# Spacing the fill matmuls anew at the head of each pair of heads, and staging the first later block through ScalarE

## What is computed

```python
hn = rms_norm(h, norm_mix_pre[l])
p = hn @ w_in[l]
p_rw, p_ret, g_rw, g_ret = _split(p, IN_SIZES)
y_rw = rwkv7_mixer(p_rw, ...)         # below
y_ret = retention_mixer(p_ret, positions)

# rwkv7_mixer, for each head, over the tokens:
kk = kk / jnp.maximum(jnp.sqrt(jnp.sum(kk * kk, axis=-1, keepdims=True)), 1e-12)
k = k * (1.0 + (a - 1.0) * k_a)
sa = jnp.einsum('bhvk,bhk->bhv', S, -kk_t)
S = S * w_t + sa[..., None] * (kk_t * a_t) + v_t[..., None] * k_t
y = jnp.einsum('bhvk,bhk->bhv', S, r_t)
bonus = jnp.sum(r * k * r_k, axis=-1, keepdims=True) * v
```

## Time and profile before

| | |
|---|---|
| median of three runs (range) | 2453.03 us (2448.63 to 2453.11) |
| the profiled execution | 2453.11 us, span 2451.3 us |
| busy: PE, DVE, POOL, ACT | 97%, 56%, 32%, 27% of the span |
| mean granted PE clock | 0.992 of full speed |
| fills (L608, L613, L615) | 1920 matmuls, 779 us busy |

### The profile page before, as it was taken

One profiled execution on the slowest core, in us unless ns is written; L12 is line 12 of the kernel. 1 busy time (PEld: TensorE's weight loads), 2 busy tenths in 40 slices (PEclk: granted clock), 3 DMA queues, 4 the chain that ended last, 5 costly groups with the idle time before them and its releaser, 6 DMA issues.

```text
span 2451.3 us, 33679 instructions
## 1 busy us (share of the span) xinstructions
PE 2377.4 (97%) x12944; PEld 1922.5 (78%) x12944; DVE 1370.6 (56%) x1562; ACT 660.1 (27%) x1064; POOL 790.9 (32%) x420
## 2 busy tenths in 40 slices
PE   7999999999999999899999999999999999999997
PEld 5788878887888788787787788888878787777775
DVE  7744374437444653676638654455451387657766
ACT  4311121112112111343224211111122445114541
POOL 2311221123123214212465433333334445422164
PEclk9999999999999999999999999999999999999998
DMA  3111211111112114654444211111124333221123
GB/s 140 58 61 44 70 52 61 52 61 53 51 52 70 61 46 149 197 175 156 158 151 134 81 43 47 47 47 47 43 60 145 120 120 100 70 63 35 35 78 112
DMA packets 61904, 205.22 MB, mean 84 GB/s; under 512 B 6240, under 2 KB 10464, under 8 KB 61152
## 3 DMA queue, kind: packets, MB, share of 16 engines
q1 hardware_dynamic: 40560, 138.76, 18.2%
q10 hardware_dynamic: 21232, 64.80, 7.2%
HBM read 167.36 MB, written 36.18 MB: 83 GB/s over the span
## 4 chain that ended last, share of the span: by engine, by line
PE 83%; DVE 10%; DVEq 2%; ACT 2%; issue 1%; POOLq 0%; DMA 0%; POOL 0%; ACTq 0%
PE psg L476 10%; PE psg L481 9%; PE psg L480 9%; PE psg L615 5%; PE psg L613 5%; PE psg L608 5%; PE psa L704 1%; PE psg L1186 1%; PE psg L1179 1%; PE psg L1184 1%; PE psb L693 1%; PE psg L1223 1%; PE psg L1229 1%; PE psg L1227 1%; PE psb L700 1%
## 5 line engine op out<-in xcount | busy, mean ns | idle before, releaser
L401 POOL CAST whi<-wraw 128x1024 fp32r<-128x1024 f32 (+1 forms) x176 | 195.2, 1109 | 1437.1 <-PE psg L608 551.1
L403 POOL TENSOR_TENSOR wlo<-wraw,whi 128x1024 fp32r<-128x1024 f32 (+1 forms) x176 | 457.2, 2598 | 25.4 <-issue 0.2
L476 PE MATMUL psg<-xhi,whi 128*128 128x512 f32 x1008 | 402.6, 399 | 3.5 <-issue 1.9
L481 PE MATMUL psg<-xhi,wlo 128*128 128x512 f32 x1008 | 397.5, 394 | 0.0
L480 PE MATMUL psg<-xlo,whi 128*128 128x512 f32 x1008 | 396.0, 393 | 0.0
L615 PE MATMUL psg<-xhi,wlo 128*128 128x512 f32 x640 | 261.2, 408 | 0.0
L608 PE MATMUL psg<-xhi,whi 128*128 128x512 f32 x640 | 259.3, 405 | 0.0
L613 PE MATMUL psg<-xlo,whi 128*128 128x512 f32 x640 | 258.5, 404 | 0.0
L476 PEld LDWEIGHTS psg<-xhi,whi 128*128 128x128 f32 x1008 | 189.2, 188 | 49.6 <-issue 5.0
L481 PEld LDWEIGHTS psg<-xhi,wlo 128*128 128x128 f32 x1008 | 189.2, 188 | 48.2
L480 PEld LDWEIGHTS psg<-xlo,whi 128*128 128x128 f32 x1008 | 189.2, 188 | 45.9 <-issue 0.7
(11 more groups left out here) (612 smaller groups left out, 4821.5 us busy)
## 6 DMA issues: line engine op xcount, KB each, us to landing
wraw<-w SPq DMA_DIRECT2D x224, 512.0 KB, 3.6
later_scratch<-stage ACTq DMA_DIRECT2D x40, 512.0 KB, 2.6
xres<-xt ACTq DMA_DIRECT2D x4, 1024.0 KB, 11.6
RV<-later_scratch SPq DMA_DIRECT2D x4, 1024.0 KB, 11.6
RG<-later_scratch SPq DMA_DIRECT2D x4, 1024.0 KB, 5.7
later_scratch<-rstage ACTq DMA_DIRECT2D x8, 512.0 KB, 2.7
mgr<-later_scratch ACTq DMA_DIRECT2D x8, 512.0 KB, 3.6
mgt<-later_scratch ACTq DMA_DIRECT2D x8, 512.0 KB, 4.5
```

The source lines that it names most:

```text
L401: pool.tensor_copy(whi[:, u, 0:width], wraw[:, u, 0:width])
L403: pool.tensor_tensor(wlo[:, u, 0:width], wraw[:, u, 0:width], whi[:, u, 0:width].bitcast(F32), ALU.subtract).then_inc(w_ready, 1)
L476: mm = pe.matmul(ps[:, cols], whi[:, slot, w_cols], rhs_hi(k, cols), start=(k == 0), stop=False)
L481: mm = pe.matmul(ps[:, cols], wlo[:, slot, w_cols], rhs_hi(k, cols), start=False, stop=(k == kts - 1))
```

## The change

PE's 83 fills at the head of a pair, 36 before the wait on `hd_exp`, 14 before that on `rk_prod` and 33 before that on `rw_prep`, become 10, 22 and 51.

Block 0 takes another way out of PSUM. ScalarE copies it raw from `psg[0]` to `stage` (`put_first`), behind its last exponential of the head. VectorE multiplies `stage` by `factor` in place (`staged_half`), in group 0 behind `XM` of levels 1 and 2, in place of `normed_half(0, ...)` at the head of the group. The store of block 0 is issued behind `M` of level 3. In group 0 the halves of block 1 move from levels 3 and 4 to levels 4 and 5, and its store behind the levels. ScalarE gets a wait on `pp_ready` at the start of a pair.

```diff
@@ PE
-                fill(36)
+                fill(10)
                 pe.wait_ge(sem("hd_exp"), 2 * i + 1)
                 spread(TM).then_inc(sem("hd_rep"), 1)
-                fill(14)
+                fill(22)
                 pe.wait_ge(sem("rk_prod"), i + 1)
                 sum_rows(psb, M_BLK, TM).then_inc(sem("bonus_sum"), 1)
-                fill(33)
+                fill(51)
                 pe.wait_ge(sem("rw_prep"), i + 1)
@@ VectorE
+                def staged_half(half):
+
+                    cols = slice(half * HALF, (half + 1) * HALF)
+                    if half == 0:
+                        v.wait_ge(g_free[0], 8 * i + 6)
+                    mm = tt(stage[:, cols], stage[:, cols], factor[:, cols], MUL)
+                    if half:
+                        mm.then_inc(sem("first_normed"), 1)
...
                 tt(BON[:, :], flat(psb), V[:, :], MUL).then_inc(sem("rw_prep"), 1)
-                for half in range(2):
-                    normed_half(0, half)
                 for g in range(GROUPS):
...
-                        if lv in (3, 4):
-                            normed_half(2 * g + 1, lv - 3)
+                        if g == 0 and lv in (1, 2):
+                            staged_half(lv - 1)
+                        if lv in ((3, 4) if g else (4, 5)):
+                            normed_half(2 * g + 1, lv - (3 if g else 4))
@@ ScalarE
+                def put_first():
+                    s.wait_ge(sem("stored1"), 80 * i + 16)
+                    s.wait_ge(g_full, T_RW + RW_T * i + 7)
+                    act(stage[:, :], psg[0][:, :], CP).then_inc(g_free[0], 1)
+
+                s.wait_ge(sem("pp_ready"), i + 2)
...
                 act(SG[:, :], SG[:, :], EXP, scale=-C0).then_inc(sem("exp_ready"), 1)
-                store_later(0)
+                put_first()
                 for g in range(GROUPS):
...
-                        if lv == 4:
+                        if g == 0 and lv == 3:
+                            s.wait_ge(sem("first_normed"), i + 1)
+                            store_later(0)
+                        if g and lv == 4:
                             store_later(2 * g + 1)
+                    if g == 0:
+                        store_later(1)
```

## The result

The changed kernel takes 2474.12 us (median of four runs, 2473.2 to 2476.04) against 2453.07 before: ratio 1.0091, interval 1.0074 to 1.0108, so 18 to 26 us slower. A second set beside other kernels, with the label `again`, gave 2472.37 us, ratio 1.0086 (1.0072 to 1.0100). The profiled execution took 2471.75 us, span 2470.0, mean granted clock 0.990.

The account below looks back on a forecast made before the run. PE, busy 97% of the span, was taken to bound the kernel. Shift 12.8 + clock 4.8 - drops 3.4 + 0 + collision 4.0 = +18.2 us on 2453.11 gave 2471 us, range 2462 to 2475.

Parts of the forecast that it names:

- the clock: Head of each pair: low clock on the fills behind PE's idle time, 1.2 us per pair, 4.8 in all.
- the collision: Level 1, group 0: staged half waits for GpSimd's subtraction, L693 starts 1.0 us late per pair, 4.0 in all.
- the shift: Head of each pair: PE waits 5.7 us for TM, group 0 starts 3.2 us later, 12.8 in all.
- the drops taken away: Group 0: three drops of the granted clock behind the BON wait, 1.13 us each, disappear; 3.4 us less.
- The halves at the head of group 0: Head of group 0: taking the two normed_half(0, ...) away is worth 0 to PE.
- a stretched product: Level 1 of group 0: the staged half takes 1.9 us under GpSimd's subtraction, making L693 0.15 us late.
- The stores: Stores of blocks 0 and 1 in group 0: their later issue costs 0, with 0.2 us of cover.
- (b): Rival, chance 0.06: no wait at hd_exp; the BON waits and three drops are pure gain, 2439 us.
- (c): Rival, chance 0.07: GpSimd's split misses the mixing of V, hd_exp comes 2.2 us earlier, about 2457 us.
- (a): Rival, chance 0.27: level-1 half only stretched or ahead of GpSimd, 0 to 0.6 us, about 2467 to 2468.

Follow-up runs that it names:

- warm: Changed kernel plus 24 extra matmuls, whose result nobody reads, after the tenth fill, so PE is busy while it waits for TM: 2464.80 us, ratio 1.0050.
- fills: Kernel before with only the fills moved to 10/22/51, block 0 leaving PSUM as before: 2466.44 us, ratio 1.0056.
- stage23: Changed kernel with fills back at 36/14/33 and staged halves at levels 2 and 3 in place of 1 and 2: 2452.47 us, ratio 0.9997.
- lv23: Changed kernel with its two staged halves behind XM of levels 2 and 3 in place of 1 and 2: 2467.56 us, ratio 1.0058.
- hold: Kernel before, but GpSimd waits for rw_prep of the pair before it splits the weights of block f=2: 2437.39 us, ratio 0.9933.

## Where the prediction was off, and what it had right

The direction and the mechanism were right at each step, but one term was too small, and the range ended too low for it. The medians, 2474.1 and 2472.4, are 1 to 3 us above the 2471 forecast, and the ratio of the first set, put on 2453, reads 2475.4: just past the upper end of 2475.

That the profiled execution, at 2471.75 us, came within 1 us of the forecast is luck. At the head and in group 0, where the whole sum plays, it lost 21.7 us against the 18.2 forecast; it was 3.1 us quicker elsewhere, for which the sum has no term. The 3.5 between 18.2 and 21.7 are 2.6 from the clock, 0.8 from the collision and 0.3 from the shift, less 0.2 from the drops taken away.

- *The shift.* Forecast +3.2 us per pair, measured 3.27 (warm). The signal for `TM` did not move, PE stood 5.6 us before it, and the wait for `BON` went.
- *The clock: the step that failed, by its size.* "Bounds 0 and 1.55, I take 1.2." It was 1.3, 2.2, 2.6 and 1.4 us in the four pairs, 7.4 in place of 4.8, and two of the four lie outside the bounds. The upper bound took for granted that a low stretch lasts 3.4 us, as those behind the short waits in group 0 did. Behind 5.6 us of idle time it lasted 6.8 us in pairs 1 and 2, and in pair 2 PE ran 5.4 us of work at 0.50, in one piece. With PE kept busy in the wait (`warm`) the 7.4 are gone and the shift stays. With the term at 7.4 the sum is 12.8 + 7.4 - 3.4 + 4.0 = +20.8, and the time 2474. Why the stretch is 3.4 us long behind one such wait and 6.8 behind the next stays open.
- *The drops taken away.* Forecast -3.4; `fills`, where nothing else touches group 0, gives -3.6.
- *The halves at the head of group 0.* Forecast 0; `stage23` gives 0.
- *The collision at level 1.* Forecast 1.0 per pair, measured 1.2, the upper bound. L693 lists 0.91 of wait, counted from the modelled end of the fill before it. By the starts it comes 1.31 us behind that fill, where it came 0.24 behind it before: 1.07 of the 1.2. The alternative, a stretched product, would have been 0.15. VectorE's half began 0.14 us behind GpSimd and lasted to 124.27, when GpSimd was done at 123.73 which leaves 0.54 of its own 0.68. The rule of the Trainium skill, "SBUF — State Buffer", section "Who interferes with whom", that the later of the two is blocked until the earlier is done, agrees with this trace to 0.14 us.
- *The stores.* Forecast 0: VectorE waited 0.2 us per pair for the landing of store 0, inside its gap. `lv23`, which has the same stores, bounds all of it at 0.07 us per pair.
- *The rivals.* (b) and (c) needed an earlier `TM`; it came within 0.1 us of the old place. (a) fell with the 2.79. A slip in (b), on which nothing rests: the point where it decides is 5.7 - 2.6 = 3.1 us, not 3.3.

What I had read and not followed up: the slow L1462 and L1464. I wrote that nobody waits for what their speed-up frees, which is right for the changed kernel. In the kernel before, their 3.0 us of extra length were the whole of the wait for `BON`, as `hold` shows.

## What to carry to other kernels

Work that covers a wait is worth its full length where it stands ahead of the wait, and nothing behind it; before moving it towards the wait that the profile lists, look up how much slack the unlisted waits have (0.3 us here). Ask of a listed wait first what made the awaited engine late: two products at 1.7 and 2.8 times their length, under another engine's burst that could as well come later, were worth 15 us. An idle time of PE costs itself and then the low clock behind it: 7.4 us behind the four waits of 5.6 us here, another third.

## What the hardware showed that I had not expected

The low clock behind an idle time is not one fixed charge. Behind waits of 2.6 us it came once or not at all and cost 1.1 to 1.6 us. Behind waits of 5.6 us it came all sixteen times (four pairs each in the traces of the changed kernel, `again`, `fills` and `lv23`), for 3.4 or 6.8 us, and cost 1.3 to 2.7. Matmuls whose result nobody reads, issued during the wait, kept the clock at 2.4 GHz and gave back 7.6 us against `again` (7.1 with each against its own set), while `spread` started where it had before, 8.2 to 8.3 us behind the first fill.
